# Latent attention: TensorE's order of work within each unit's turn

## What is computed

```
kv = (ckv_all @ P['mla_w_ukv'][l]).reshape(B, S, MLA_HEADS, MLA_NOPE + MLA_V)
k_nope = rms_norm(kv[..., :MLA_NOPE], P['mla_kn_nope'][l])
v = kv[..., MLA_NOPE:]
k = concat(k_nope, k_rope shared by the 8 heads); q likewise from the query latent
s = einsum('bqhd,bshd->bhqs', q, k) * (q.shape[-1] ** -0.5)
p = softmax(where(k_pos // 64 <= q_pos // 64, s, NEG_BIG))
o = einsum('bhqs,bshd->bqhd', p, v)
```

## Time and profile before

| | |
|---|---|
| median of the three runs | 5863.43 us |
| the profiled execution's own time | 5870.41 us |
| its span, first to last instruction | 5868.8 us |
| PE busy over the span | 5148.0 us (88%) |
| DVE, ACT, POOL busy | 2007.4, 1426.0, 129.4 us |
| mean granted clock of TensorE | 0.928 |

### The profile page before, as it was taken

The page is one execution under the profiler, slowest core; times in us unless marked ns, Lnnn a source line. Parts: engine busy times, 40 slices in busy tenths (PEclk is TensorE's granted clock), DMA queues, the critical chain, the costliest instruction groups (busy, mean ns, idle before and its releaser), DMA issues. The chain is left out here.

```text
span 5868.8 us, 64080 instructions
## 1 busy us (share of the span) xinstructions
PE 5148.0 (88%) x25008; PEld 3340.1 (57%) x25008; DVE 2007.4 (34%) x4108; ACT 1426.0 (24%) x3278; POOL 129.4 (2%) x370
## 2 busy tenths in 40 slices
PE   5798978887988998999957988888879889989999
PEld 2466565654665664555424664656546656655554
DVE  2244344314552442011123453433145524420111
ACT  1222222113552331000012222211135523310000
POOL 0000000000000000000000000000000000100000
PEclk8899989788999999999978999997989999999999
DMA  4000000021002111111130000000210011111111
GB/s 172 20 21 7 21 20 14 4 86 36 20 15 71 49 45 55 68 63 43 50 134 20 21 7 21 24 10 4 86 38 17 16 70 58 38 59 63 63 43 54
DMA packets 122558, 253.40 MB, mean 43 GB/s; under 512 B 50772, under 2 KB 72532, under 8 KB 117030
## 3 DMA queue, kind: packets, MB, share of 16 engines
q1 hardware_dynamic: 122136, 244.48, 12.2%
q10 hardware_dynamic: 112, 4.72, 0.2%
HBM read 201.83 MB, written 52.06 MB: 43 GB/s over the span
## 5 line engine op out<-in xcount | busy, mean ns | idle before, releaser
L2220 PE MATMUL banks<-hT,w_gate 128*128 128x384 f32 x2304 | 771.7, 488 | 28.0 <-DMA w_branch<-in_w_br 28.0
L2220 PEld LDWEIGHTS banks<-hT,w_gate 128*128 128x128 f32 x2304 | 439.9, 191 | 335.8 <-DMA w_branch<-in_w_br 28.5
L847 PE MATMUL banks<-hT,w_piece 128*128 128x384 f32 x1536 | 552.6, 502 | 0.2
L1985 PE MATMUL banks<-hT,w_piece 128*128 128x384 f32 x1152 | 389.0, 493 | 16.7 <-DMA w_piece<-in_w_cols 15.2
L2222 PE MATMUL banks<-y_branch,w_branch 128*128 128x384 f32 x1152 | 395.1, 486 | 0.0
L847 PEld LDWEIGHTS banks<-hT,w_piece 128*128 128x128 f32 x1536 | 278.6, 192 | 187.2 <-issue 24.0
L2243 ACT ACTIVATE gate_tanh<-banks 128x384 f32<-128x384 f32 x144 | 70.8, 492 | 1077.6 <-PE banks L2222 1077.6
L1985 PEld LDWEIGHTS banks<-hT,w_piece 128*128 128x128 f32 x1152 | 218.4, 194 | 157.1 <-DMA w_piece<-in_w_cols 15.7
L2222 PEld LDWEIGHTS banks<-y_branch,w_branch 128*128 128x128 f32 x1152 | 218.9, 190 | 152.6
L2256 DVE SCALAR_TENSOR_TENSOR gate_tanh<-gate_tanh,banks 128x384 f32<-128x384 f32 x96 | 53.2, 554 | 634.1 <-ACT gate_tanh L2243 634.1
L2234 PE MATMUL banks<-w_out,mergedT 128*128 128x512 f32 x576 | 247.5, 592 | 0.0
(11 more groups left out here) (315 smaller groups left out, 8166.5 us busy)
## 6 DMA issues: line engine op xcount, KB each, us to landing
w_piece<-in_w_cols SPq DMA_DIRECT2D x64, 512.0 KB, 4.2
w_ada<-in_w_ada SPq DMA_DIRECT2D x12, 2048.0 KB, 9.7
w_gate<-in_w_cols SPq DMA_DIRECT2D x48, 512.0 KB, 3.4
y_branch<-y_gated SPq DMA_DIRECT2D x6, 2304.0 KB
w_branch<-in_w_br SPq DMA_DIRECT2D x48, 256.0 KB, 3.6
x_rows<-out_y_prompt SPq DMA_DIRECT2D x2, 4096.0 KB, 21.3
sb_cached_keysT<-in_sbkT SPq DMA_DIRECT2D x8, 1024.0 KB, 7.2
sb_cached_values<-in_sbv SPq DMA_DIRECT2D x8, 1024.0 KB, 5.3
```

What stands on the lines that cost most here:

```text
L847: last = mm(dst, w[0 if kind in ("z", "r") else 1][:, k, :], hT[:, k, c], start=(k == 0), stop=(k == KD - 1))
L1985: last = mm(ps[:, bank[n], 0:TG], w[wn % 3][:, k, :], hT[:, k, TG * g:TG * g + TG], start=(k == 0), stop=(k == KD - 1))
L2220: nc.tensor.matmul(ps[:, 2 * (u % 4), 0:TG], wg[j % 2][:, k, :], hT[:, k, c], start=(k == 0), stop=(k == KD - 1))
```

## The change

TensorE's turn in the loop over the units is written in another order. Before it is: `raw`, `scores(u + 2)`, `turns(u)`, `value_rows`, `values(u - 1)`, `sums`. Now it is: `turns(u)`, `raw`, `values(u - 1)`, `scores(u + 2)`, `value_rows`, `sums`. All waits stand inside these functions and move with them. The programs of DVE, ACT, POOL and SP stay as they are, row for row.

```diff
             for u in range(U + 1):
                 mine = at_step[u]
+                if u < U:
+                    turns(u)
                 for n in mine:
                     if fills[n][0] == "norm":
                         raw(n)
+                values(u - 1)
                 scores(u + 2)
-                if u < U:
-                    turns(u)
                 for n in mine:
                     if fills[n][0] == "value":
                         value_rows(n)
-                values(u - 1)
                 for n in mine:
                     if fills[n][0] == "norm":
                         sums(n)
```

## The result

The changed kernel took 6116.97 us (median of four runs, 6107.03 to 6121.91) against 5862.24 us before: ratio 1.0432, 95% interval 1.0413 to 1.045. That is slower, as forecast, by 255 us where 177 were forecast, and 7 us above the top of the range.

What follows compares the result with a forecast made beforehand. PE's instruction stream was taken as the bound (busy 281.24 of 315 us in the loop). Profiled 5870.4 + 144 for waits + 33 for the clock = 6047; that execution being 7 above the median, forecast 6040 us, range 5970 to 6110.

Steps and rivals of the forecast that it cites:

- D: Delay from the end of scores(u + 2) to turns(u + 1), through DVE's maximum and scaling; 2.71 us read at W = 7.
- term 1: Before the transposes: D loses its cover, bare but for 0.53 us of sums, or 2.32 with value_rows; whole in the last pair.
- Terms 2 and 3: W = 8 to 5: raw ahead of products leaves PE idle 1.15 us (0.36 before); odd turns' second transposes wait 0.65 to 0.5.
- the ring: Odd turns' second transpose group waits for ACT to free the bank of values(u - 1): 0.65 to 0.5 us, W = 8 to 5.
- The first rival: Half of it is hidden: hand-overs in the loop are faster, without 37 us of effects 2 and 3; 5972 us, chance 0.13.
- Term 4: Value fill in step 14 (W = 2): its 1.89 us wait for DVE's norm goes, as it stands a turn's work later.
- Sum of the waits: Loop over units: the four effects without the clock, +72 us for one layer, +144 us for two.
- Term 5, the clock: Some 25 new PE gaps per layer, 1.3 us per clock fall; half taken, 33 us, of at most 65.
- The third rival: The clock stays low: 1.2 GHz for a third of the pairs with fills, all the last pair; +190, 6197 us, chance 0.1.
- its sign, a loop clock under 0.8: In the profile after, a granted clock under 0.8 over the loop would show that the third rival holds.

## Why the prediction missed

*D and its cover, term 1: right.* D for the odd turn of W = 7 was 2.52 us worked out and 2.51 measured. Both turns of W = 7 take 16.3 us (1614.79 to 1631.08), and 14.8 without their slow stretch, where 14.7 were forecast. Pair 1 takes 112.9 us after (1597.49 to 1710.41), 103.6 were forecast for the waits alone; its slow stretches, measured against the same matmuls in the run with all gaps filled, are 1.9 us at W = 8, 1.5 at W = 7 and about 4.9 at the sample units. Without them it is 104.6. The last pair, with the clock held up, took 59.3 against 57.8.

*Terms 2 and 3: right in kind, a little large.* The products waited 0.96 (1.15 forecast), the ring 0.43 (0.6). Alone, the move of `raw` costs nothing. (The first rival's 37 us for these two terms do not follow from its own 0.8 and 0.6 us in 24 pairs of turns; those make 34.)

*Term 4: right.* The value fills waited 16.8 us for DVE's norm before, and 0.0 after.

*Sum of the waits:* 144 us forecast, 133 in the trace.

*Term 5, the clock: the step that failed.* It was taken as 33 us, half of 25 gaps a layer at 1.3 us each; the trace has 112 us, and filling the gaps gave 86 back. Three things were mis-sized. A fall costs 1.5 to 1.9 us in a turn with fills, not 1.3. At each pair's start, where the sample units' gaps follow one another, it is nearly 5 us; the forecast held those gaps as waits of D and gave them no fall. And the first layer's last pair lost 15 us (74.3 against 59.3), at a granted clock of 0.70. The price of 1.3 us had been read from single gaps inside dense work, and neither place is like that. Nor is "half of the gaps" a rule that the traces bear out: in the pairs with fills slow matmuls followed the gap of 1.92 us at W = 7 in all six cases of the two layers and that of 1.72 at W = 6 in one of six, yet in the last pair the transposes and scores behind the gap of 2.42 us (odd turn of W = 7) ran at full speed in both layers. What decides it beside the gap's length stays open.

The third rival (190 us for the clock, the last pair wholly slow) had the mechanism, but its 190 us are 1.7 times what the trace has, and its sign, a loop clock under 0.8, was not met (0.85); the truth lay between it and the forecast. The loop took about 440 us where 390 to 405 were expected. The range's top, 6110 us, held all 25 falls a layer at 1.3 us (65 us) and 38 us more, together still less than the clock took.

## What to carry to other kernels

Where engines run hand-written loops in order, look for what stands ahead of the awaited instruction on its engine: here unit u + 1 waited for the maximum of unit u + 2, on DVE and behind it again on ACT, and only work placed between the two on PE hid that. Move no producer to the end of a turn whose next turn begins with the consumer. When a change opens gaps on TensorE, read the price of the slow matmuls behind them from a stretch with gaps like the new ones, and not from a single gap in a dense stream, or widen the range where there is no such stretch; a run that fills the gaps with useless matmuls tells waiting from clock.

## What was not expected of the hardware

Useless matmuls made the kernel faster, by 64 us in one run and 86 in the other. A gap's length did not tell what follows: 1.92 us was followed by slow matmuls six times of six and 1.72 once of six, but one of 2.42 us in the last pair was not, in either layer. And doubling a DVE reduction in the kernel before cost 68 us, of which only 16 are new waits of the transposes; 29 are PE's longer busy time, and new waits for ACT's copy of the value fills, 24 us, account for the rest.
